# A hybrid encoder trunk on TensorE: its first two units and a last row interleaved, the SSD scan's tile reordered, and the skip term D·x made by products with diagonals

## What is computed

```python
def swiglu(x, w_gu, w_down):
    gate, up = jnp.split(x @ w_gu, 2, axis=-1)
    return (jax.nn.silu(gate) * up) @ w_down

# ssd_scan, one chunk of 64 frames
cum = jnp.cumsum(dtb * a, axis=1)
decay = masked_decay(cum[:, :, None] - cum[:, None, :], mask)
xdt = xb * dtb[..., None]
cbs = jnp.einsum('bign,bjgn->bijg', cb, bb)
y = jnp.einsum('bijg,bijgh,bjghp->bighp', cbs, decay, xdt)
y = y + jnp.einsum('bign,bghpn,bigh->bighp', cb, h, jnp.exp(cum))
# mixer_ab, after the scan: the skip term, the gate, the norm
y = (y + p['ssm_d'][j][:, None] * xs).reshape(bsz, t, D_A) * jax.nn.silu(z.astype(F32))
y = rms_norm(y.reshape(bsz, t, G_A, D_A // G_A), ...)

# trunk, each layer l
h = h + 0.5 * swiglu(rms_norm(h, p['norm_ffn1'][l]), p['ffn1_w_gu'][l], p['ffn1_w_down'][l])
h = h + mixer(rms_norm(h, p['norm_mix'][l]))
h = h + 0.5 * swiglu(rms_norm(h, p['norm_ffn2'][l]), p['ffn2_w_gu'][l], p['ffn2_w_down'][l])
```

## Time and profile before

| | us |
|---|---|
| median of 3 runs (2495.53 to 2498.21) | 2495.88 |
| the profiled execution's own time | 2493.55 |
| its span in the trace | 2491.8 |
| PE busy (97% of the span) | 2413.3 |
| DVE busy (51%) | 1269.3 |
| ACT busy (39%) | 973.0 |
| POOL busy (1%) | 17.8 |
| PE work in the chain that ended last | 82% |

### The profile page before, as it was taken

The page is one execution under the profiler, slowest core; times in us unless marked ns, Lnnn a source line. Parts: engine busy times, 40 slices in busy tenths (PEclk is TensorE's granted clock), DMA queues, the critical chain, the costliest instruction groups (busy, mean ns, idle before and its releaser), DMA issues.

```text
span 2491.8 us, 52742 instructions
## 1 busy us (share of the span) xinstructions
PE 2413.3 (97%) x21427; PEld 2383.0 (96%) x21427; DVE 1269.3 (51%) x1857; ACT 973.0 (39%) x1393; POOL 17.8 (1%) x52
## 2 busy tenths in 40 slices
PE   7999999998999999999999999999999998999998
PEld 7999999988899999999999999999999988999998
DVE  4442444778576564433444442444777755442443
ACT  4431223566345444322234321224677734331222
POOL 2000000000000000000000000000000000000000
PEclk9999999999999999999999999999999998999999
DMA  4232232332422223332232232232222222332331
GB/s 122 84 110 68 86 104 63 98 110 69 110 75 59 76 80 93 93 93 76 86 91 85 84 109 68 86 98 80 64 67 67 60 70 68 91 107 64 93 94 52
DMA packets 396032, 208.82 MB, mean 84 GB/s; under 512 B 10015, under 2 KB 392086, under 8 KB 395894
## 3 DMA queue, kind: packets, MB, share of 16 engines
q1 hardware_dynamic: 390318, 203.11, 28.4%
q10 hardware_dynamic: 5576, 3.77, 0.5%
HBM read 201.41 MB, written 5.45 MB: 83 GB/s over the span
## 4 chain that ended last, share of the span: by engine, by line
PE 82%; DVE 8%; ACT 4%; DVEq 2%; issue 2%; ACTq 2%; DMA 0%; POOL 0%; SPq 0%; POOLq 0%
PE PD L1873 68%; PE PD L1900 9%; DVE wlo L1125 1%; DVE c_xl L1618 1%; DVEq L1619 1%; DVE CV L1301 1%; DVE c_xl L1594 0%; DVEq L1596 0%; DVE c_bw L1579 0%; ACT L483 0%; ACT L640 0%; ACTq L884 0%; PE PM L2238 0%; PE PM L2251 0%; ACT whi L493 0%
## 5 line engine op out<-in xcount | busy, mean ns | idle before, releaser
L493 ACT ACTIVATE whi<-raw 128x1024 fp32r<-128x1024 f32 (+4 forms) x348 | 381.3, 1096 | 1041.3 <-PE PD L1873 912.0
L1873 PE MATMUL PD<-XH,whi 128*128 128x272 f32 x2944 | 611.3, 289 | 3.0 <-ACT RS L528 1.5
L1873 PE MATMUL PD<-XL,whi 128*128 128x272 f32 x2944 | 608.9, 288 | 0.0
L1873 PE MATMUL PD<-XH,wlo 128*128 128x272 f32 x2944 | 607.2, 288 | 0.0
L1873 PEld LDWEIGHTS PD<-XH,whi 128*128 128x128 f32 x2944 | 462.5, 189 | 4.4 <-ACT RS L528 2.0
L1873 PEld LDWEIGHTS PD<-XL,whi 128*128 128x128 f32 x2944 | 463.8, 189 | 0.0
L1873 PEld LDWEIGHTS PD<-XH,wlo 128*128 128x128 f32 x2944 | 461.7, 189 | 0.0
L1873 PE MATMUL PD<-AH,whi 128*128 128x272 f32 x1408 | 290.6, 288 | 0.0
L1873 PE MATMUL PD<-AL,whi 128*128 128x272 f32 x1408 | 290.2, 288 | 0.0
L1873 PE MATMUL PD<-AH,wlo 128*128 128x272 f32 x1408 | 289.8, 287 | 0.0
L1137 DVE TENSOR_TENSOR wlo<-raw,whi 128x1024 fp32r<-128x1024 f32 (+2 forms) x172 | 222.6, 1294 | 105.3 <-ACT whi L493 103.9
(11 more groups left out here) (411 smaller groups left out, 2440.1 us busy)
## 6 DMA issues: line engine op xcount, KB each, us to landing
raw<-in_ffn_w_gu SPq DMA_DIRECT2D x176, 512.0 KB, 3.8
raw<-in_ffn_w_down SPq DMA_DIRECT2D x32, 768.0 KB, 4.8
raw<-in_ab_w_in SPq DMA_DIRECT2D x44, 512.0 KB, 3.9
raw<-in_ffn_w_down SPq DMA_DIRECT2D x32, 640.0 KB, 4.4
raw<-in_c_w_in SPq DMA_DIRECT2D x32, 512.0 KB, 4.1
LM<-cum_rows SPq DMA_DIRECT2D x8, 512.0 KB, 5.1
raw<-in_ab_w_out SPq DMA_DIRECT2D x16, 256.0 KB, 2.9
raw<-in_ab_w_out SPq DMA_DIRECT2D x8, 512.0 KB, 4.0
```

The source lines that it names most:

```text
L493: A(whi[ps % 2][:, 0:k, :], raw[ps % 4][:, 0:k, :], ACT.Copy).then_inc(S["hi_ready"], 1)
L1873: last = mm(PD[:, 2 * (ps % 2) + s, 0:HT], wt[ps % 2][:, r, :], x[:, r, s * HT:(s + 1) * HT], start=(p == 0 and q == 0), stop=(p == 2 and ...
```

## The change

**Start.** SP issues x part 0, x_sample, part 1, the weights of unit 0, parts 2 and 3, the weights of unit 1, and then eleven small tables; only norm_ffn1 (16 rows) is issued by ACT, after its table load. PE makes 12 transposes of the identity while it waits. The high products of units 0 and 1 (`high_rows`: whi·XH and whi·XL) are woven with the transposes, the low ones (`low_rows`) follow; wlo of both comes from DVE. `rms_columns` stands before unit 1's low products, the remaining small tables are turned after it. On ACT, after x0, x1, the weights of unit 0 and x2, the squares and XH tiles alternate, with unit 1's weights after x4. The lower-bound arithmetic of HGRN2 moves to ahead of l0f2. One place on PE (buffer numbers stand behind the names: whi_56 and whi_57 are units 0 and 1), from unit 0's first row on, before:

The diff, cut to its core:

```diff
@@ SP, start (new; load(b, b, ...) fetches unit b) @@
+                part(0)
+                sp.dma_start(xin[0:TS, NC, :], a["x_sample"].rearrange("b t d -> (b t) d")).then_inc(x_landed[4], 16)
+                part(1)
+                weight(0)
+                part(2)
+                part(3)
+                weight(1)
...
@@ ACT, start @@
-            for m in range(3):
-                first_x(m)
+            first_x(0)
+            first_x(1)
+            first_w(0)
+            first_x(2)
             for q in range(5):
                 act.wait_ge(x_landed[q], 16)
             token_squares(0)
             first_x(3)
-            first_w(0)
             token_squares(1)
             first_x(4)
+            first_w(1)
...
@@ ACT, start, later @@
+            hi(2, 0, KT)
             act.wait_ge(S["rs_psum"], 1)
@@ PE, start (new) @@
+            def high_rows(u, r):
+
+                if r == 0:
+                    pe.wait_ge(S["hi_ready"], u + 1)
                 pe.wait_ge(S["xh_ready"], r + 1)
                 pe.wait_ge(S["xl_ready"], r + 1)
+                for p, x in enumerate((XH, XL)):
+                    for s in range(2):
+                        mm(PD[:, 2 * u + s, 0:HT], whi[u][:, r, :], x[:, r, s * HT:(s + 1) * HT], start=(p == 0 and r == 0), stop=False)
...
+            for r in range(4):
+                high_rows(1, r)
+            for r in range(4, 6):
+                high_rows(0, r)
+                high_rows(1, r)
+            low_rows(0, 0, 6)
+            for r in range(6, KT):
+                high_rows(0, r)
+                high_rows(1, r)
+            low_rows(0, 6, KT)
             rms_columns()
-            unit(1, 0, KT, XH, XL)
+            low_rows(1, 0, KT)
+            late_rows()
             run_rest("l0f1_up0", XH, XL)
@@ DVE, one tile's output @@
                 TT(ep, PM[:, 1, TS:TS + T - CH], ep, ALU.mult)
-                STT(y, XX[:, j % 2, :], DCOL[:, j:j + 1], PM[:, 0:2, :].rearrange("p s t -> p (s t)")[:, 0:T], ALU.mult, ALU.add)
                 dve.drain()
-                TT(y[:, CH:T], y[:, CH:T], ep, ALU.add)
+                TT(y, EP[:, :], PM[:, 0:2, :].rearrange("p s t -> p (s t)")[:, 0:T], ALU.add)
@@ DVE, the scan's tiles @@
                 gate_row(m - 1)
                 inputs(m - 1)
+                lo(ux + 2 * m + 1)
@@ PE, run @@
                 if after_first:
+                    unit_rows(u0 + 1, 0, 3, k, rh, rl)
                     after_first()
-                if n > 1:
+                    unit_rows(u0 + 1, 3, k, k, rh, rl)
+                    run_rest(name, rh, rl)
+                elif n > 1:
@@ PE, outputs @@
+                    for e, es in enumerate(halves):
+                        mm(PM[es, 0, cs], XD[:, c, es], LM[:, e, c, :], start=True, stop=False)
+                    for es in halves:
+                        mm(PM[es, 0, cs], DDG[j // 4][:, j % 4, es], XX[:, j % 2, cs], start=False, stop=True)
@@ PE, end of the scan @@
-            out_rows(0, 0, 3, True)
+            for r in range(4):
+                out_rows(0, r, r + 1, True)
+            out_rows(1, 0, 4)
             turn(j)
-            out_rows(0, 3, 4, True)
-            out_rows(1, 0, 3)
+            out_rows(2, 0, 2)
             products(j)
@@ PE, last row @@
+            for q in range(OPEN - 1):
+                last_row(q)
+            ps = plan["c_rest"][0]
+            unit_rows(ps, 0, 2, KT, COH, COL)
+            last_row(OPEN - 1)
+            unit_rows(ps, 2, KT, KT, COH, COL)
+            unit_rows(ps + 1, 0, KT, KT, COH, COL)
@@ DVE, last row @@
+                whole(OPEN, plan["c_first"][0])
+                last_row(0)
+                last_row(1)
+                low(8, 7)
+                last_row(2)
+                last_row(3)
+                last_row(4)
+                x_lows(0, 2)
+                low(8, 8)
+                squares(0, 1)
...
```

More of the change, by code:

```diff
@@ L53 @@
 OPEN = 5
-ORDER = list(range(OPEN, KT)) + list(range(OPEN))
+ORDER = [OPEN] + list(range(OPEN)) + list(range(OPEN + 1, KT))
 def dense_plan():
@@ L790, in _ @@
             decay(0)
-            for m in range(1, KT):
+            for m in range(1, KT - 1):
                 weights(ux + 2 * m + 2)
@@ L805, in _ @@
             j = KT - 1
+            weights(uy)
+            for n in range(4):
+                y_high(n)
+            first_tap(4 + j)
+            square(j - 2)
+            weights(uy + 1)
+            square(j - 1)
+            silu_set()
+            z_silu(j)
             differences(j)
             weights(uy + 2)
+            conv_silu(4 + j)
+            weights(uy + 3)
             logs_set()
@@ L810, in _ @@
             spreads(j)
-            weights(uy + 3)
-            square(j - 1)
             weights(uy + 4)
@@ L1208, in body @@
                                 up(None, u0 + b, b)
[L1209 removed]
+                                if t or b or not skip:
+                                    lo_ahead(u0, 2 * t + b, i, k, last)
                             hold("dve", S["silu_done"], 2 * i + (base + t + 1))
@@ new lines, in x_lows, with squares @@
+                def x_lows(t0, t1):
+                    for turn in range(t0, t1):
+                        x_low(5, ORDER[turn], turn)
+                def squares(t0, t1):
+                    for turn in range(t0, t1):
+                        dve.wait_ge(S["sq_ready"], turn + (5 * KT - 7))
+                        TT(ACC[:, :], ACC[:, :], (SQ, CM["e1"])[turn % 2][:, :], ALU.add)
+                        dve.drain().then_inc(S["acc_done"], 1)
+                whole(OPEN, plan["c_first"][0])
@@ new lines, in last_hgrn @@
+                last_row(0)
[7 more added lines that the diff above has]
+                squares(0, 1)
+                x_lows(2, 4)
+                squares(1, 2)
+                x_lows(4, 6)
+                low(8, 9)
+                whole(6, plan["c_rest"][0])
+                squares(2, 3)
+                x_lows(6, 7)
+                squares(3, 4)
@@ L1840, in last_hgrn @@
+                whole(7, plan["c_rest"][0] + 1)
+                squares(4, 5)
+                x_lows(7, 8)
                 low(8, 10)
+                squares(5, 8)
                 states_stored(4 + KT)
```

370 lines of the change are left out of this document (213 added, 157 removed).

## The result

| | before | after |
|---|---|---|
| median of the runs, us | 2495.70 (4 runs, 2493.55 to 2498.21) | 2472.90 (4 runs, 2471.23 to 2478.47) |
| the profiled execution's own time | 2493.55 | 2471.36 |
| its span | 2491.8 | 2469.6 |
| PE busy | 2413.3 | 2409.1 |

The ratio is 0.9917 with a 95% interval of 0.9900 to 0.9933. The forecast was 2472.6, faster; the span fell by 22.2 us against a summed 23.3. That the total fits says little about the terms, so marks of PE's list are laid side by side. The two columns are starts in the two traces, the last is what the stretch ending there gave or took.

The account below looks back on a forecast made before the run. PE was taken to bound the kernel, busy 2413.3 of 2491.8 us. Terms summed to -23.3, so 2493.55 became 2470.2; the median, 2.3 above, gave 2472.6, range 2462 to 2485 with rivals.

Parts of the forecast that it names:

- Start: From kernel start to unit 2: x complete at 12.0, ACT's last XH at 22.4, unit 2 at 30.5; -12.0 us.
- Ahead of tile 0: Before the first scan tile: PE's 0.65 us wait for DVE goes, the eight diagonals take part back; -1.0 us.
- Scan tiles: Tile 0's turn to tile 6's: added products 1.11 us per tile, EP delay 2.1, 112.5 against 108.2; +4.3 us.
- Its first part: In the scan: DVE's saving is not on PE's path, added products make a floor tile 18.4, six 110.4 us.
- The second step: In the scan: the gate unit's low part some 2 us later holds SP's weight load and EP's fetch; 2.1 us added.
- End of the scan: From tile 6's turn, into ab_outy0: two units ahead of the last turn cover low parts and convolution; -6.9 us.
- Squares later: In l0f2 and l1f1: the squares' sum three rows later, 2.26 us against 0.6 slack, 1.7 wait each; +3.7 us.
- the next term: Last row and start of l1f2, -11.4 us; l1f2's wait from the later squares was counted inside it.
- Last row: Last row and start of l1f2: rows of tiles 6 and 7 cover waits, 5.6 of 17.5 us left; -11.4 us.

## Why the prediction was right, and where its steps were not

**Start (forecast -12.0, measured -13.4).** The mechanism held: x complete, then ACT's alternation, then PE. x was 0.8 later than assumed and ACT's last XH 0.6. The mis-sized term is the clock: I let 20 of 80 products go at half clock, and none did. From unit 1's first product to unit 2's, the rms columns and late tables with them, PE took 11.8 us where I had 13.5.

**Ahead of tile 0 (-1.0, -1.6).** As forecast. That the diagonals cost DVE 1.66 us in a place where PE is waiting is seen only where the reordering is missing.

**Scan tiles (+4.3, +5.2).** The sum was near for a partly wrong reason. Its first part says that DVE's saving is not on PE's path, and that fell: with DVE's pass back and 5.9 us of products gone from PE, the six periods were not shorter (114.05 against 113.35, and 109.48 against 109.43), and ACT waited longer for DVE's convolution. The working also takes all six tiles at the floor of the wait, 110.4, although before they stood 4.4 above it (108.20 against six of 17.3), and gives no reason. That is what came, 109.4 without the delay, with every XX wait at 1.02; by the step before it, only PE's later arrival could have done it, and DVE's lighter list has a part. That one step was wrong and the sum near is luck. The products were sized 1.11 and take 0.99, and the floor after the change is 18.04 where I had 18.4, with 19.13 for the sixth period. The second step, the fetch of EP held back by the late low part, I priced at 2.1; it costs 3.9, of which some 1.6 is the one clock fall. The kernel before, at 108.20, is 1.2 better than all six kernels without the delay (109.40 to 109.48). The one among them with the skip term on DVE had two clock falls in these periods, the kernel before one; whether that is its order or its run is not settled.

**End of the scan (-6.9, -8.5).** The wait for YL shrank to 1.59 where I left 2.8, and no clock fall followed, where I left 1.5. Together 2.7, more than the 1.6 that the term was off.

**Squares later (+3.7, two waits of 1.95 and 1.87).** The slack read from three rows (0.6 us against a move of 2.26) gave 1.7 each, right to 0.3. The step that failed is the one after it: the third such wait, in l1f2, was not "inside the next term" but an own wait of 1.85, with a clock fall behind it. The wait stands in the -12.4, the fall is the +1.4 at the end of the table. Undoing it gave 3.7 us.

**Last row (-11.4, -12.4).** The size held, the terms less. I had left 1.3 for an XL, 0.65 for a low part, 1.6 for the sum of squares and 2 for a clock fall; what is left is 0.3, 0.8, nothing and no fall inside the stretch, 0.3 at a last row, and the 1.85 of l1f2's third unit. I put the gain down to the rows of tiles 6 and 7; by the rows, the waits between the last rows themselves went with DVE's order.

**Not forecast: the GLA stage,** where nothing was changed. From the GLA's first turn to the first unit of its output projection it took 167.17 us before and 169.21 after; the other kernels with the changed start and scan spread from 167.3 to 169.6. PE's waits ahead of the GLA's level products in this stage, before and then after:

```profile
PE PM L2229 <- issue: 0.7, 2, 0.4
```
```profile
PE PM L2393 <- issue: 2.3, 4, 0.8
```
They are 1.6 of the 2.0 us, and the profile names no releaser for them. I have no cause for it beyond that, and it took back 2 us that the other terms had given above the forecast. The agreement of the total to 0.3 us owes as much to this as to the working.

## To carry to other kernels

Before moving a sum, a split or a fetch later, follow what stands behind it in every queue that it releases, SP's included: here a low part made 2 us later held back a load, the load a small fetch, the fetch ACT, and 3.9 us were lost on an engine three steps away. An operation moved from a helping engine to the bounding one costs nothing only if the helper's time was on the path; the wait at the join, above its floor, says how much is to be had, and it should be read before the sum is made. Where a wait near 2 us is left, its price is the wait and, in some runs, a clock fall behind it.

## What the runs showed of the hardware

- A record of a plain fp32 product of 128 columns took 0.11 us at full width and 0.055 at 64 output channels (halves in turn). Products of the two widths in alternation cost 0.79 us per chunk where the same work in one width cost 0.43. Widths are better grouped.
- Waits of 1.85 to 2.8 us were followed by a stretch at 1.2 GHz in some places and not in others of the same length: behind 1.95 us in l0f2 not in the profiled run of the changed kernel nor in the one with the low part early, but in those of seven variants, with 3.2 to 3.5 us at half rate. Behind 2.80 us in the scan it was at half rate for 3.4 us.
- At the start the clock was at its upper level from 6.5 us on when PE turned the identity ahead of x, and from 11.5 us without.
- In l0f2 identical pairs went at 0.2502 us in some runs and at 0.2509 in others, both at a granted clock of 1.00; over 397 us that is 1.2.
